# Moving the raw loads and the stores of a weight-sum stage from SyncE's queue to GpSimd's

## The reference, cut to what matters

```
proj = rmsnorm(h) @ w_in            # q, k, v, g of every head
o    = normed(retention(q, k, v))   # chunkwise-recurrent
h    = h + (o * silu(g)) @ w_out
```

## Time and profile before

| | us |
|---|---|
| median of 3 runs | 2471.71 |
| lowest, highest | 2467.61, 2475.48 |
| profiled execution, its time | 2471.62 |
| its span, first to last instruction | 2469.8 |

### The profile page before, as it was taken

The page is one execution under the profiler, slowest core; times in us unless marked ns, Lnnn a source line. Parts: engine busy times, 40 slices in busy tenths (PEclk is TensorE's granted clock), DMA queues, the critical chain, the costliest instruction groups (busy, mean ns, idle before and its releaser), DMA issues.

```text
span 2469.8 us, 28619 instructions
## 1 busy us (share of the span) xinstructions
PE 2410.3 (98%) x11264; PEld 1978.4 (80%) x11264; DVE 1431.9 (58%) x2010; ACT 666.7 (27%) x1450; POOL 414.3 (17%) x310
## 2 busy tenths in 40 slices
PE   7999999999989999999999999999999999999998
PEld 6888888877768787878888888888888887888886
DVE  6555655677545545553758564655567745657374
ACT  2212312235121211121442231223352212313143
POOL 2111111221244545430001000000001100001000
PEclk9999999999999999999999999999999999999999
DMA  8667565645698898975259878775447977787433
GB/s 349 269 230 289 208 255 228 232 183 210 247 351 329 316 350 306 358 253 189 101 207 324 275 251 290 246 258 211 149 163 234 334 263 272 255 277 251 171 103 145
DMA packets 126393, 613.25 MB, mean 248 GB/s; under 512 B 8544, under 2 KB 9312, under 8 KB 104288
## 3 DMA queue, kind: packets, MB, share of 16 engines
q1 hardware_dynamic: 117424, 575.94, 64.5%
q10 hardware_dynamic: 8880, 36.18, 3.9%
HBM read 459.00 MB, written 153.09 MB: 248 GB/s over the span
## 4 chain that ended last, share of the span: by engine, by line
PE 83%; DVE 9%; DMA 4%; issue 2%; ACT 1%; POOL 1%; SPq 1%; DVEq 0%; ACTq 0%; POOLq 0%
PE ps L674 26%; PE ps L676 26%; PE ps L675 26%; DMA whl<-split_w 2%; PE ps L1127 2%; DVE ff L1857 1%; DMA comb_w<-ff 1%; DVE ff L2077 1%; PE ps L1137 1%; DVE ff L1965 1%; DVE fr L1556 1%; PE ps L935 1%; PE ps L822 1%; ACT ff L1424 1%; DVE mx L2117 1%
## 5 line engine op out<-in xcount | busy, mean ns | idle before, releaser
L674 PE MATMUL ps<-whl,xhi 128*128 128x512 f32 (+1 forms) x1088 | 418.4, 385 | 11.3 <-DMA whl<-split_w 6.9
L676 PE MATMUL ps<-whl,xlo 128*128 128x512 f32 (+1 forms) x1088 | 412.8, 379 | 0.0
L675 PE MATMUL ps<-whl,xhi 128*128 128x512 f32 (+1 forms) x1088 | 411.6, 378 | 0.0
L674 PE MATMUL ps<-xhi,whl 128*128 128x512 f32 x768 | 305.4, 398 | 21.6 <-DVE xlo L1560 16.2
L676 PE MATMUL ps<-xhi,whl 128*128 128x512 f32 x768 | 301.4, 392 | 0.0
L675 PE MATMUL ps<-xlo,whl 128*128 128x512 f32 x768 | 300.9, 392 | 0.0
L674 PE MATMUL ps<-whl,fr 128*128 128x512 f32 x704 | 282.1, 401 | 2.4 <-DVE whl L1598 2.1
L676 PE MATMUL ps<-whl,fr 128*128 128x512 f32 x704 | 278.8, 396 | 0.0
L675 PE MATMUL ps<-whl,fr 128*128 128x512 f32 x704 | 278.4, 395 | 0.0
L674 PEld LDWEIGHTS ps<-whl,xhi 128*128 128x128 f32 x1088 | 205.7, 189 | 50.4 <-DMA whl<-split_w 7.4
L676 PEld LDWEIGHTS ps<-whl,xlo 128*128 128x128 f32 x1088 | 205.5, 189 | 38.9
(11 more groups left out here) (199 smaller groups left out, 3703.3 us busy)
## 6 DMA issues: line engine op xcount, KB each, us to landing
whl<-split_w SPq DMA_DIRECT2D x68, 2048.0 KB, 8.6
whl<-split_w SPq DMA_DIRECT2D x110, 1024.0 KB, 6.8
split_w<-whl SPq DMA_DIRECT2D x44, 2048.0 KB, 7.2
whl<-vg_w SPq DMA_DIRECT2D x64, 1024.0 KB, 6.7
raw<-in_stream SPq DMA_DIRECT2D x44, 1024.0 KB, 9.4
vg_w<-ff SPq DMA_DIRECT2D x32, 1024.0 KB, 8.3
raw<-in_stream SPq DMA_DIRECT2D x50, 512.0 KB, 9.5
whl<-comb_w SPq DMA_DIRECT2D x24, 1024.0 KB, 6.4
```

Source lines behind the costliest of these rows:

```text
L674: pe.matmul(dst, lhs[0], rhs[0], start=start, stop=False)
L675: pe.matmul(dst, lhs[0], rhs[1], start=False, stop=False)
L676: return pe.matmul(dst, lhs[1], rhs[0], start=False, stop=stop)
```

## The change

SyncE issues only the chunk loads in block 1: `combining_head` becomes a loop of 8 `load_split` calls. `load_piece` and `store_piece` move into GpSimd's program, with the same sources, destinations and sizes, issued by `pool.dma_start`. `comb_piece` now ends with `store_piece(at, j)`: GpSimd waits for `comb_lo` of piece j, issues its two stores, and then the two raw loads of the piece two later. The first two pieces are loaded by GpSimd after block 0's work. `post_loads` loses the parameter for the last store.

```diff
-                if h == 0:
-                    load_piece(0, 0)
-                    load_piece(0, 1)
-                for c in range(3):
+                for c in range(8):
                     load_split(at, c, split_rows(h, c), CHUNK)
-                    if c == 1 and h > 0:
-                        last_store()
-                        load_piece(h, 1)
-                store_piece(0)
-                load_piece(h, 2)
-                load_split(at, 3, split_rows(h, 3), CHUNK)
-                store_piece(1)
-                load_piece(h, 3)
...
+            def store_piece(at, j):
+                h = at.h
+                pool.wait_ge(comb_lo.sem, at(comb_lo, j + 1))
+                for i in range(2):
...
+                    pool.dma_start(dst.rearrange("(q p) n -> p q n", p=P),
+                                   stage[:, i, :].rearrange("p (q n) -> p q n", q=4)).then_inc(comb_stored.sem, 16)
+                if j + 2 < PIECES:
+                    load_piece(h, j + 2)
+                elif h < HEADS - 1:
+                    load_piece(h + 1, j + 2 - PIECES)
...
                 if own_lo:
                     pool.wait_ge(comb_hi.sem, at(comb_hi, j + 1))
                     pool.tensor_tensor(stage[:, 1, :].bitcast(F32R), raw[j % 2], stage[:, 0, :], ALU.subtract).then_inc(comb_lo.sem, 1)
+                store_piece(at, j)
...
+            for i in range(2):
+                pool.wait_ge(w_ready[i].sem, 16 * (BLOCK_CHUNKS // 2))
+            load_piece(0, 0)
+            load_piece(0, 1)
```

More of the change, by code:

```diff
@@ L445, in comb_rows, with combining_head @@
                 return comb_w[(4 * h + q) * P:(4 * h + q + 1) * P, :, :]
-            def combining_head(b, h, last_store=None):
+            def combining_head(b, h):
                 at = Place("head", b, h)
[L450 to L474, removed]
-                if h == 0:
-                    load_piece(0, 0)
-                    load_piece(0, 1)
-                for c in range(3):
-                    load_split(at, c, split_rows(h, c), CHUNK)
-                    if c == 1 and h > 0:
-                        last_store()
-                        load_piece(h, 1)
-                store_piece(0)
-                load_piece(h, 2)
-                load_split(at, 3, split_rows(h, 3), CHUNK)
-                store_piece(1)
-                load_piece(h, 3)
[L489 to L500, removed]
@@ L525, in fast_head, with post_loads @@
                     sp.dma_start(slot[j % 4].bitcast(F32), src).then_inc(half_ready[j % 4].sem, 16)
-            def post_loads(b, last_store=None):
+            def post_loads(b):
                 at = Place("post", b)
@@ L537, in post_loads @@
                                  split_w[n * P:(n + 1) * P, :, 0:width(n)]).then_inc(ready[c % 2].sem, 16)
-                    if c == 1 and last_store is not None:
-                        last_store()
-            last_store = None
             for h in range(HEADS):
-                last_store = combining_head(1, h, last_store)
-            post_loads(1, last_store)
+                combining_head(1, h)
+            post_loads(1)
             sp.wait_ge(comb_stored.sem, Place("head", 1, HEADS - 1)(comb_stored, 2 * PIECES))
@@ L611, in _, with load_piece @@
             h_root(Place("post", 0), 2)
+            def load_piece(h, j):
+                for i in range(2):
+                    if j < 2:
+                        n = h * HEAD_CHUNKS + 6 + i
+                        src = stream[n * P:(n + 1) * P, :].rearrange("p (a i n) -> p a i n", a=2, i=2)[:, :, j, :]
+                    else:
+                        n = h * HEAD_CHUNKS + 2 + 2 * i
+                        src = stream[n * P:(n + 2) * P, (j - 2) * 512:(j - 1) * 512].rearrange("(c p) n -> p c n", p=P)
+                    pool.dma_start(raw[j % 2][:, i * HALF:(i + 1) * HALF].rearrange("p (a n) -> p a n", a=2), src).then_inc(comb_raw[j % 2].sem, 16)
+            def store_piece(at, j):
+                h = at.h
+                pool.wait_ge(comb_lo.sem, at(comb_lo, j + 1))
+                for i in range(2):
+                    if j < 2:
+                        dst = comb_w[4 * h * P:4 * (h + 1) * P, i, j * 512:(j + 1) * 512]
+                    else:
+                        dst = vg_w[4 * h * P:4 * (h + 1) * P, i, (j - 2) * 512:(j - 1) * 512]
+                    pool.dma_start(dst.rearrange("(q p) n -> p q n", p=P),
[4 more added lines that the diff above has]
+                    load_piece(h + 1, j + 2 - PIECES)
             def comb_piece(at, j, own_lo=False):
```

## The result

The changed kernel takes 2654.63 us (median of 4 runs, 2651.57 to 2655.72) against 2470.31 for the kernel before: ratio 1.0741, 95% interval 1.0721 to 1.0762. It is 184 us slower. I had forecast slower, by 36 us, with a range up to 2575; the direction was right, the size five times too small.

What follows compares the result with a forecast made beforehand. TensorE, busy 98% of the span, was taken as the bound, with block 1's low-part chain setting its time. Heads 1 to 3 lose 36.6 us, head 0 gains 1.0: 35.6 on 2471.62 gives 2507 us, range 2470 to 2575.

Steps and rivals of the forecast that it cites:

- the chain: Block 1's sequence low part, stores, rounding, low part, said to set TensorE's time already, with about 0.1 us slack.
- half clock: TensorE at clock 0.50 behind a long v_lo wait in block 1, put at 1.6 us a head in heads 1 to 3.
- H: Time GpSimd is held after each block 1 low part by two stores and two raw loads; taken as 6 us.
- a rival with 0.22: In block 1 GpSimd is held until stores have drained: H = 8 gives 2538 us, H = 12 gives 2598; chance 0.22.
- Head 0's 7 us: At block 1's start, chunk 0's product ends 7 us earlier, so VectorE comes for the low part at 664.0, not 671.04.
- H + 11.0 and order: In block 1, differences behind GpSimd's low-part wait make the low-part cycle 17.1 us at H = 6, instead of 12.8 and 13.3.
- H = 3.4 decides: Break-even for block 1: at H = 3.4 three heads lose 8.4 us, head 0 gains 9, no change; smaller is faster.
- Stores land later: Rival: block 1 stores beside chunk 3 on another queue take 14.7 us; +53 us, 2525 us; chance 0.13.
- the 4.00 us at the block's start: TensorE's wait before block 1's first product, to be won as chunk 0 no longer stands behind four raw loads.

Runs made afterwards that it cites:

- e1: The changed kernel with dynamic_dma_scratch_size 2048 instead of 1024, nothing else: 2495.55 us, ratio 1.0100.
- e3: The kernel before with one added wait: GpSimd waits for piece j's low part before piece j+1's differences, all DMAs staying with SyncE: 2470.45 us, ratio 0.9998.
- e6: Against the kernel before, only the raw loads move to GpSimd; SyncE keeps stores and chunk loads, scratch 1024: 2482.19 us, ratio 1.0043.
- e5: Against the kernel before, only the stores move to GpSimd; SyncE keeps raw loads and chunk loads, scratch 1024: 2645.07 us, ratio 1.0697.
- e2: The changed kernel, scratch 1024, with stores written in one run of 8 KB per partition instead of four of 2 KB: 2489.48 us, ratio 1.0077.
- e7: The changed kernel with dynamic_dma_scratch_size 1088 instead of 1024: 2600.95 us (one run).
- e8: The changed kernel with scratch 2048, SyncE issuing chunk 3 of each head only when piece 0's stores have landed: 2502.13 us, ratio 1.0123.

## Why lateness reaches TensorE, and a version that is faster than both

In the prediction the chain cost TensorE time because `v_lo` stands behind the low part of piece 2. Test on e1: VectorE takes `v_lo` first.

```diff
-                    if combine:
-                        comb_less_hi(2)
                     for t in range(TT):
                         dve.wait_ge(v_hi.sem, at(v_hi, t + 1))
                         scaled_less_hi(vhl[1][:, t, :], ps[:, t, :], vcol[:, h, t:t + 1], vhl[0][:, t, :], v_lo)
+                    if combine:
+                        comb_less_hi(2)
```

> As e1 (changed kernel, scratch 2048), and VectorE takes the four v_lo parts before the low part of piece 2 instead of after it. Theory (a late chain costs TensorE time only because v_lo stands behind the low part of piece 2): e1's 32.3 us of waits for v_lo fall below 8 us, and the time falls from 2495 to 2465 to 2478. Rival (the low part of piece 1, ahead of the transposed k and the scores, holds update(0) and inner(0) just as much): TensorE's wait moves to kt_lo or s_lo and the time stays above 2485.

2470.83 us, ratio 0.9999 (0.9989 to 1.0009): all of e1's remaining 24 us come back. TensorE's waits, e1 first, then this kernel:

```profile
PE ps L653 <- DVE fr L1539: 32.3, 4, 9.9
PE ps L801 <- DVE ff L1944: 8.7, 8, 1.5
```

```profile
PE ps L801 <- DVE ff L1944: 9.1, 8, 1.9
PE ps L653 <- DVE fr L1539: 6.0, 5, 1.6
```

The stores land as late as in e1 (14.2 us for piece 0 in head 1), but nobody on TensorE's path waits for them. What is left is mainly `o_root` behind GpSimd's four issues. Putting it first (only the lines of GpSimd's program that differ from e10; `store=False` skips the call of `store_piece`):

```diff
-                        for j in range(4):
-                            comb_piece(at, j)
+                        for j in range(4):
+                            comb_piece(at, j, store=j < 3)
                     o_root(at)
                     if b < FAST:
+                        store_piece(at, 3)
                         comb_piece(at, 4, True)
```

> As e10 (changed kernel, scratch 2048, v_lo before the low part of piece 2), and GpSimd does o_root before it issues the stores and loads of piece 3, not after. Theory: o_root loses the part of the issue time that reaches past VectorE's variance, 1.1 us in each of the four heads; TensorE's first wait for transposes of y goes from 1.4 back to 0.3 us and the time falls by 4 us from e10's 2470.8, to 2466 to 2468, level with e9. Rival (the stores of piece 3, issued 3 us later, delay piece 4 and with it the head's end or the next head): no gain, 2470 us or more.

2465.01 us, ratio 0.9970 (0.9958 to 0.9982), 1 us better than the lower end expected. It was measured at another time than e10, so the 5.8 us between the two medians are less sure than each ratio to the kernel before. Its waits for the transposes of y are gone from the list.

Two smaller versions start from the kernel before. In e4, SyncE issues chunk 0 of block 1 ahead of the raw loads:

```diff
-                if h == 0:
-                    load_piece(0, 0)
-                    load_piece(0, 1)
                 for c in range(3):
                     load_split(at, c, split_rows(h, c), CHUNK)
+                    if c == 0 and h == 0:
+                        load_piece(0, 0)
+                        load_piece(0, 1)
```

> The kernel before with one thing moved: at the start of block 1 SyncE issues chunk 0 before the four raw loads, everything else as before. Theory: TensorE's 4.00 us wait at the block's start and the 3 us of half clock behind it go, and as all of head 0's later chain moves with them the time falls by about 7 us, to 2464. Rival (the low parts chain of head 0 takes it all back, as in the changed kernel): within 2 us of before.

2465.94 us, ratio 0.9977 (0.9968 to 0.9987). The 4 us wait goes. A new one of 1.5 us for VectorE's line 1870, the k product again, stands in head 0, probably because `final_norm` on VectorE does not move with the rest; the gain is 5.4 us, not 7.

e9 adds `v_lo` first, e11 moves the low part of piece 2 one step later still, behind `statistics(0)`:

> As e4 (the kernel before with chunk 0 issued ahead of the raw loads), with the same move on VectorE: v_lo before the low part of piece 2. Theory: head 0's wait of 4.5 us for v_lo with its half clock goes, in the other heads nothing is late, so about 5 us are won on e4: 2458 to 2463 us. Rival (the low part then stands in front of the state update, which has no slack): 1 to 2 us lost in each head, 2465 us or more.

> As e9, but the low part of piece 2 comes one step later still, behind the first state update and statistics. Theory: the same gain as e9, 2458 to 2463 us, if the first state update is the one without slack. Rival: the second state update has none either (VectorE idles 1.2 us ahead of it, the low part takes 2.3), so 1 us a head is lost and e9 is as fast or faster.

e9: 2465.46 us, ratio 0.9980 (0.9970 to 0.9989), the same as e4 and above the 2458 to 2463 that the theory gave. TensorE's waits for `v_lo` fall from 5.0 to 1.6 us, but 2.6 us come back as waits for chunks (6.7 to 9.3): in head 0 it now comes for chunk 4 2.3 us before it has landed. e11: 2470.43 us, ratio 0.9994 (0.9985 to 1.0003), with 12.8 us of such waits in 10; one of 3.1 us in head 0 stands before chunk 6. Neither theory had named them. That SyncE issues the later chunks behind the store of piece 2, and so behind the low part that was put off, would explain e11; it was not tested by itself.

So of the versions run, the change pays only in the one with the scratch at 2048 and both reorderings: 7 us on the kernel before (e12). e4 gets 5.4 by moving two lines, and the intervals of the two overlap.

## Why the prediction was wrong

**The step that failed is H.** "I take H = 6, halfway from 4.1 to the 8 us around which stores land." It measured 11.7 us after piece 0, 16.0 after piece 1 and 20.2 after piece 5, and was never under 11.6. I priced the work of issuing, and that part was even too high (3.0 us). What holds GpSimd goes when the scratch is doubled (273 us of waits become 10.9, e1); it comes twice per piece, and each wait lasts until a DMA issued before has landed. That GpSimd is held stood in the prediction as a rival with 0.22 and a bound of 12 us. That bound was itself taken wrongly: halfway between 7.6 and 14.7 is 11.2, and nothing in the rows makes it an upper end, since it allows for one transfer and not for two in turn. From the kernel's 1024 and the 1,536 runs of 2 KB in a piece, a limit on the runs under way could have been tried as a guess, and with it two waits of at least the shortest landing each, 4.2 us. I did not try it.

**The rest of the working carries over.** With H = 15, put in afterwards and between the measured values, the same sums give: piece 0's low part 8.3 us late, piece 2's 34.2 late, half clock 1.6, `o_root` 12.7, the last three together 48.5 us a head; measured 49.8. The wait for the k product that I had not named comes from the first of these. Half clock was sized at 1.6 for one wait; with three waits a head it cost about 6, which the 48.5 does not hold, so its close fit is in part luck.

**Head 0's 7 us.** The forecast has VectorE come for piece 0's low part 7 us earlier than 671.04; no run shows that term. It comes 5.2 us earlier in the changed kernel (665.85) and 4.2 in e4 (666.81). TensorE's part of it is there: its first two products start 5.7 us earlier (640.17 against 645.88) and take 21.8 us instead of 24.8, at a granted clock of 1.00 from 646 to 652 instead of 0.50.

**"H + 11.0 and order".** The order itself is free (e3), as the differences fit into the stores' landing. In e1 H measured 3.5 us (786.17 to 789.62; 3.0 of issuing and the hand-over). There the cycle from piece 0 to piece 1 is not set by H + 11.0 = 14.5 but by landing stores: 16.7 us between the two low parts, plus 2.3. The break-even "H = 3.4 decides" was therefore wrong too: at 3.5 the kernel was still 24 us slower. So the direction came out right partly by luck: even at the break-even the kernel is slower, for a reason that this sum does not hold.

**"Stores land later" (0.13) was right beside the other rival, not instead of it.** In head 1 of e1 they took 14.3 us against 8.0; 14.7 was the longest landing, which that rival took. With the scratch at 2048 the late chain costs 24 us (e1 to e10), and landing stores release 16 of its 24 roundings; with the raw loads alone moved the kernel is 10 us slower (e6), and stores that land late lengthen GpSimd's waits (10.8 us in the mean in e5, against 5.1).

**What held.** The chunk waits of TensorE went; the 4.00 us at the block's start were won (0.2 left); `v_lo` became the longest wait of each head (25 us in the mean, not 8), and e10 shows that the path runs through it; `o_root` delays TensorE when GpSimd's issues stand before it (the transposes wait 13.8 us in the mean, not 4; e12 against e10: 5.8 us in four heads).

## What to carry to other kernels

Before DMAs are moved to GpSimd's queue, count the runs that will be under way together: with the scratch at 1024 every DMA that would have brought them to 1,024 waited (47 in the changed kernel, 24 in e5), and GpSimd itself stood still until an earlier one had landed. With the transfers split over two queues, stores that others waited for could land later: piece 0's in head 1 were done 8.0 us after their issue with one queue, 10.1 in e6 and 14.3 in e1. And when a side chain is late, look first at which instruction on the main path stands behind it in program order; moving one call won 24 us (e10), more than any change of the order on the queues.

## What the runs showed of the hardware

- GpSimd issued a DMA of 512 runs in 0.75 to 0.85 us, one of 256 runs in 0.72 us (median) and one of 128 runs in 0.58 us (median, e2), so four times the runs cost some 0.2 us. SyncE needs 0.46 us for a store and 0.6 to 1.3 for a raw load.
- GpSimd's standstills before its DMAs show as idle time with the reason `issue`, without a semaphore: 273 us in 47 waits in the changed kernel, 11 us in 2 with the scratch at 2048 (e1). In the three kernels with such a wait in every piece (the changed one, e5, e7), all 94 end 0.31 to 0.34 us after a landing.
- A GpSimd store's landing depends on what runs beside it. Of piece 0 in head 1: 4.6 us for the first store of the changed kernel, alone; 13.4 with 3 MB beside it on SyncE's queue (e5); 11.1 and 13.3 for the pair in e1, with each other, the raw loads and chunk 3 beside them; 5.0 and 7.8 with chunk 3 held back (e8).
